# Mixture-of-experts stages on one core: weight rounding, `hidT` and row gathers in another order

## The reference, cut to what matters

```python
# top-1 of 4 groups, then top-2 of its 8 experts; pairs (token, expert)
# are sorted by expert into blocks of 128 rows, padded per expert
def run_block(args):
    xb, e = args                       # 128 rows x 1024
    hid = jax.nn.silu(xb @ w_gate[e]) * (xb @ w_up[e])     # 128 x 256
    return hid @ w_down[e]             # 128 x 1024
y = segment_sum(out[dest] * gate, token)   # added to the residual stream
```

## Time and profile before

| | us |
|---|---|
| median of three runs (3124.84 to 3132.12) | 3131.38 |
| the profiled execution | 3119.75 |
| its span in the profile | 3117.8 |
| expert stage of layer 0, about | 1188 to 1730 |
| expert stage of layer 1, about | 2588 to 3117 |

### The profile page before, as it was taken

The page is one execution under the profiler, slowest core; times in us unless marked ns, Lnnn a source line. Parts: engine busy times, 40 slices in busy tenths (PEclk is TensorE's granted clock), DMA queues, the critical chain, the costliest instruction groups (busy, mean ns, idle before and its releaser), DMA issues. The chain is left out here.

```text
span 3117.8 us, 48627 instructions
## 1 busy us (share of the span) xinstructions
PE 2673.4 (86%) x15109; PEld 2236.8 (72%) x15112; DVE 1747.1 (56%) x3154; ACT 1260.4 (40%) x2369; POOL 724.0 (23%) x923
## 2 busy tenths in 40 slices
PE   5999979997968947998898599799879947989997
PEld 4999958875847836777676488578658836767775
DVE  4222246665755665667765366588733354676664
ACT  3222132225841104556654222288611104675653
POOL 1000023321110002444343143211100002444433
PEclk9999989998988968999999799899979968999998
DMA  6111112215536516899997322222154415999995
GB/s 243 50 56 52 40 60 78 75 65 165 163 121 234 194 61 216 261 301 302 316 281 228 118 87 80 91 83 88 53 198 143 149 39 179 298 359 285 283 308 132
DMA packets 175389, 509.57 MB, mean 163 GB/s; under 512 B 53800, under 2 KB 81456, under 8 KB 150320
## 3 DMA queue, kind: packets, MB, share of 16 engines
q1 hardware_dynamic: 142480, 393.69, 34.7%
q0 software_dynamic: 32800, 114.51, 15.4%
HBM read 374.56 MB, written 133.56 MB: 163 GB/s over the span
## 5 line engine op out<-in xcount | busy, mean ns | idle before, releaser
L1700 DVE TENSOR_TENSOR moe_parts<-expert_w,moe_parts 128x1024 fp32r<-128x1024 f32 x384 | 452.3, 1221 | 238.4 <-ACT moe_parts L1649 234.9
L1582 PE MATMUL ps<-moe_parts,moe_xT 128*128 128x512 f32 x2232 | 551.6, 403 | 23.0 <-issue 16.0
L1582 PEld LDWEIGHTS ps<-moe_parts,moe_xT 128*128 128x128 f32 x2232 | 418.1, 191 | 125.3 <-issue 20.5
L1649 ACT ACTIVATE moe_parts<-expert_w 128x1024 fp32r<-128x1024 f32 x384 | 373.3, 1047 | 80.3 <-PEq L155 78.8
L1109 PE MATMUL ps<-out_w,out_catT 128*128 128x512 f32 x1344 | 322.4, 399 | 14.2 <-DVE out_w L1265 11.8
L560 PE MATMUL ps<-in_gate_w,in_gate_hnT 128*128 128x384 f32 (+1 forms) x1536 | 319.4, 367 | 7.4 <-DVE in_gate_w L679 7.4
L1582 PE MATMUL ps<-moe_parts,moe_hidT 128*128 128x512 f32 x1116 | 289.0, 408 | 26.9 <-DVE moe_hidT L1713 24.2
L560 PEld LDWEIGHTS ps<-in_gate_w,in_gate_hnT 128*128 128x128 f32 x1536 | 278.7, 190 | 37.4 <-issue 7.5
L1109 PEld LDWEIGHTS ps<-out_w,out_catT 128*128 128x128 f32 x1344 | 255.7, 192 | 69.4 <-DVE out_w L1265 12.6
L560 PE MATMUL ps<-in_qk_w,in_qk_hnT 128*128 128x512 f32 x1152 | 268.4, 394 | 9.2 <-DVE in_qk_w L679 9.2
L1582 PEld LDWEIGHTS ps<-moe_parts,moe_hidT 128*128 128x128 f32 x1116 | 205.7, 191 | 76.2 <-DVE moe_hidT L1713 32.8
(11 more groups left out here) (262 smaller groups left out, 4150.8 us busy)
## 6 DMA issues: line engine op xcount, KB each, us to landing
expert_w<-in_w_gate SPq DMA_DIRECT2D x64, 1024.0 KB
expert_w<-in_w_up SPq DMA_DIRECT2D x64, 1024.0 KB
expert_w<-in_w_down SPq DMA_DIRECT2D x64, 1024.0 KB
hn_d<-out_hn SPq DMA_DIRECT2D x32, 512.0 KB, 2.6
in_gate_xt<-in_x SPq DMA_DIRECT2D x16, 512.0 KB
in_qk_xt<-in_x SPq DMA_DIRECT2D x16, 512.0 KB
att_k<-k_d SPq DMA_DIRECT2D x64, 128.0 KB, 2.9
out_ht<-in_x SPq DMA_DIRECT2D x16, 512.0 KB, 4.6
```

Of the source, the lines that this page charges most:

```text
L1582: last = nc.tensor.matmul(out, left[:, a, k, :], right(b, k), start=(n == 0 and k == 0), stop=(n == 2 and k == K_ - 1))
L1649: nc.scalar.activation(parts[:, j, 0, at], K.expert_w[:, j, at], ACT.Copy).then_inc(w_high.sem, 1)
L1700: nc.vector.tensor_tensor(parts[:, j, 1, at], K.expert_w[:, j, at], parts[:, j, 0, at].bitcast(F32), ALU.subtract).then_inc(w_low.sem, 1)
```

## The change

- Weights: `load_expert` becomes `load_up` (gate and up) and `load_down`, each with its own semaphores. The down weights of an expert are split in that expert's own first block, no longer in the one before, and loaded accordingly.
- ScalarE's order in a block becomes `act(m-1)`, `x_out(m)`, `hid_out(m-1)`, `y_scaled(m-2)`, with the pieces of weights between them; the rounding of `hidT` is ScalarE's, the subtraction stays VectorE's.
- `raise_` and `lower` begin when the high part is there and wait for the low part before the last third of their matmuls.
- The gather takes its indices from `K.where` with a bounds check that drops rows past 2047; `K.who` is gone. `xg` is cleared once.
- `y_scaled` reads its gate straight from `K.gates`, which has a leading column of zeros; `set_gate` is gone. One extra `y_scaled(-1)` runs at the start and isn't scattered.

The core of the diff (the `who` and `gates` allocations, `load_up` and `load_down` themselves and unchanged lines are left out):

```diff
         def _(sp):
             def load(i, j):
 
-                load_expert(K, sp, layer, i * 2 + j, j, lambda n: alone(
-                    sp, w_low, i * (2 * PIECES) + ((j - 2) * PIECES + (n + 1) * PIECES // 3), K.tick_sp))
-            with sp.Fori(1, NE // 2) as i:
+                if not (isinstance(i, int) and i == 0 and j == 0):
+                    alone(sp, Count(d_low), (i * 2 + j) * D_PIECES, K.tick_sp)
+                    load_down(K, sp, layer, i * 2 + j + 1, 1 - j)
+                load_up(K, sp, layer, i * 2 + j + 2, j, lambda n: alone(
+                    sp, Count(gu_low), (i * 2 + j) * GU_PIECES + (n + 1) * GU_PIECES // 2, K.tick_sp))
+            for j in range(2):
+                load(0, j)
+            with sp.Fori(1, NE // 2 - 1) as i:
                 for j in range(2):
                     load(i, j)
+            alone(sp, Count(d_low), (NE - 2) * D_PIECES, K.tick_sp)
+            load_down(K, sp, layer, NE - 1, 1)
             if layer == 0:
 
-                sp.wait_ge(w_low.sem, NE * PIECES)
+                sp.wait_ge(gu_low, NE * GU_PIECES)
+                sp.wait_ge(d_low, NE * D_PIECES)
                 sp.dma_start(K.w_in_odd, K.x["w_in_odd"].rearrange("a (p k) n -> p (a k) n", k=DK)).then_inc(K.weights_in[5], 16)
...
             def gather(m):
-                nc.gpsimd.tensor_copy(who[:, :], K.who[:, m:m + 1] if isinstance(m, int) else K.who[:, bass.ds(m, 1)]).then_inc(who_set.sem, 1)
+                nc.gpsimd.tensor_copy(who[:, :], K.where[:, m:m + 1] if isinstance(m, int) else K.where[:, bass.ds(m, 1)]).then_inc(who_set.sem, 1)
                 alone(g, who_set, m + 1, K.tick)
                 nc.gpsimd.indirect_dma_start(xg[:, :], None, K.hn_d[layer],
-                                             bass.IndirectOffsetOnAxis(ap=who[:, :], axis=0)).then_inc(gathered_s, 16)
-
-            def set_gate(m):
-                nc.gpsimd.tensor_copy(gate[:, :], K.gates[:, bass.ds(m, 1)]).then_inc(gated.sem, 1)
+                                             bass.IndirectOffsetOnAxis(ap=who[:, :], axis=0),
+                                             bounds_check=T - 1, oob_is_err=False).then_inc(gathered_s, 16)
...
+            g.memset(xg[:, :], 0.0).then_inc(cleared, 1)
+            g.wait_ge(cleared, 1)
             gather(0)
 
-            g.dma_start(where[:, :], K.where[:, 0:1]).then_inc(scattered_s, 16)
+            for n in range(2):
+                g.dma_start(where[:, :], K.where[:, 0:1]).then_inc(scattered_s, 16)
+                g.wait_ge(scattered_s, 16 * (n + 1))
...
             with g.Fori(1, total) as m:
-                set_gate(m - 1)
-
                 alone(g, x_turned, m + 2, K.tick)
                 gather(m + 2)
                 scatter(m - 1)
-            set_gate(total - 1)
...
-            def product(out, left, right, K_):
-
-                for n, (a, b) in enumerate(((0, 0), (0, 1), (1, 0))):
+            def product(out, left, right, K_, terms):
+
+                for a, b in terms:
                     for k in range(K_):
-                        last = nc.tensor.matmul(out, left[:, a, k, :], right(b, k), start=(n == 0 and k == 0),
-                                                stop=(n == 2 and k == K_ - 1))
+                        last = nc.tensor.matmul(out, left[:, a, k, :], right(b, k), start=(a + b + k == 0),
+                                                stop=(a == 1 and k == K_ - 1))
                 return last
...
             def raise_(m, j):
 
                 wgu = parts[:, j, :, 0:GU].rearrange("p h (s k f) -> p h k s f", s=2, k=DK)
+                until(pe, x_high, m + 1)
+
+                until(pe, hid_done, m)
+                product(gup, xT, lambda h, k: wgu[:, h, k, :, :], DK, ((0, 0), (0, 1)))
                 until(pe, x_low, m + 1)
...
             def lower(m, j):
 
                 wd = parts[:, j, :, GU:EW].rearrange("p h (k n) -> p h k n", k=2)
-                until(pe, h_low, m + 1)
-                until(pe, y_out, m)
-                for half in range(2):
-                    last = product(yp[:, 512 * half:512 * (half + 1)], hidT,
-                                   lambda h, k: wd[:, h, k, 512 * half:512 * (half + 1)], 2)
+                until(pe, h_high, m + 1)
+                until(pe, y_out, m + 1)
+                for terms in (((0, 0), (0, 1)), ((1, 0),)):
+                    if terms[0][0] == 1:
+                        until(pe, h_low, m + 1)
+                    for half in range(2):
+                        last = product(yp[:, 512 * half:512 * (half + 1)], hidT,
+                                       lambda h, k: wd[:, h, k, 512 * half:512 * (half + 1)], 2, terms)
                 last.then_inc(down.sem, 1)
...
-                pe.wait_ge(w_low.sem, i * (2 * PIECES) + j * PIECES + GU_PIECES)
+                pe.wait_ge(gu_low, i * (2 * GU_PIECES) + (j + 1) * GU_PIECES)
                 raise_(m, j)
                 turn_x(m + 1)
                 if behind:
+                    pe.wait_ge(d_low, i * (2 * D_PIECES) + j * D_PIECES)
                     lower(m - 1, 1 - j)
-                pe.wait_ge(w_low.sem, i * (2 * PIECES) + (j + 1) * PIECES)
...
+            def block_(i, j, m):
                 turn_hid(m - 1)
                 raise_(m, j)
                 turn_x(m + 1)
+                pe.wait_ge(d_low, i * (2 * D_PIECES) + (j + 1) * D_PIECES)
                 lower(m - 1, j)
+            pe.sem_inc(down.sem, down.credit)
             turn_x(0)
             in_turn(pe, first_block, block_)
             total = end_of(pe, NE)
             turn_hid(total - 1)
+            pe.wait_ge(d_low, NE * D_PIECES)
             lower(total - 1, 1)
...
+            def split_up(j, pieces):
                 for n in pieces:
                     at = slice(n * PIECE, (n + 1) * PIECE)
-                    nc.scalar.activation(parts[:, j, 0, at], K.expert_w[:, j, at], ACT.Copy).then_inc(w_high.sem, 1)
+                    nc.scalar.activation(parts[:, j, 0, at], K.expert_w[:, j, at], ACT.Copy).then_inc(gu_high, 1)
+
+            def split_down(i, j):
+                a.wait_ge(K.down_in[layer][j], i * 16 + 16)
+                for n in range(GU_PIECES, GU_PIECES + D_PIECES):
+                    at = slice(n * PIECE, (n + 1) * PIECE)
+                    nc.scalar.activation(parts[:, j, 0, at], K.expert_w[:, j, at], ACT.Copy).then_inc(d_high, 1)
...
+            def hid_out(m):
+                until(a, h_turned, m + 1)
+                nc.scalar.activation(hidT[:, 0, :, :], hp.rearrange("p (k c) -> p k c", k=2), ACT.Copy).then_inc(h_high.sem, 1)
+
             def y_scaled(m):
                 until(a, down, m + 1)
-                until(a, gated, m + 1)
-
-                a.wait_ge(scattered_s, m * 16 + 16)
-                nc.scalar.activation(y[:, :], yp, ACT.Copy, scale=gate[:, 0:1]).then_inc(y_out.sem, 1)
+
+                a.wait_ge(scattered_s, m * 16 + 32)
+                column = K.gates[:, m + 1:m + 2] if isinstance(m, int) else K.gates[:, bass.ds(m + 1, 1)]
+                nc.scalar.activation(y[:, :], yp, ACT.Copy, scale=column).then_inc(y_out.sem, 1)
 
             def first_block(i, j, m, behind, ahead):
                 ni, nj = i + j, 1 - j
+                if behind:
+                    act(m - 1)
                 if ahead:
-
-                    a.wait_ge(K.expert_in[layer][nj], ni * 48 + 48)
-                    if behind:
-                        until(a, up, m)
-                    split(ni, nj, range(GU_PIECES))
-                act(m)
-                x_out(m + 1)
+                    a.wait_ge(K.up_in[layer][nj], ni * 32 + 32)
+                    split_up(nj, (0,))
+                x_out(m)
                 if behind:
-                    y_scaled(m - 1)
+                    hid_out(m - 1)
                 if ahead:
-                    split(ni, nj, range(GU_PIECES, PIECES))
-
-            def block_(m, j):
-                act(m)
-                x_out(m + 1)
-                y_scaled(m - 1)
-            a.wait_ge(K.expert_in[layer][0], 48)
-            split(0, 0, range(PIECES))
-            x_out(0)
+                    split_up(nj, (1,))
+                if behind:
+                    y_scaled(m - 2)
+                split_down(i, j)
+                if ahead:
+                    split_up(nj, range(2, GU_PIECES))
+
+            def block_(i, j, m):
+                act(m - 1)
+                x_out(m)
+                hid_out(m - 1)
+                y_scaled(m - 2)
+            a.wait_ge(K.up_in[layer][0], 32)
+            split_up(0, range(GU_PIECES))
             in_turn(a, first_block, block_)
-            y_scaled(end_of(a, NE) - 1)
+            total = end_of(a, NE)
+            act(total - 1)
+            hid_out(total - 1)
+            y_scaled(total - 2)
+            y_scaled(total - 1)
 
         @block.vector
         def _(v):
             v.sem_inc(hid_done.sem, hid_done.credit)
 
-            def split(i, j, pieces):
-
+            def rest(j, n, done):
```

(46 more changed lines are left out.)

50 lines of the change are left out of this document (20 added, 30 removed).

## The result

The kernel after takes 3156.44 us in the median (3147.94 to 3157.27) beside 3128.11 for the kernel before measured next to it, a ratio of 1.0096 with the 95% interval [1.0078, 1.0114]. I had forecast 3109 us, with a range that ended at 3144. The profiled execution has a span of 3145.8 us beside 3117.8: 28 us more.

The account below looks back on a forecast made before the run. TensorE and the DMA engines were each taken to bound some blocks, DMA in runs of one-block experts. Terms -14 - 2 + 0 - 3 + 3 - 2.4 - 5 + 1 = -22.4 us from 3131.4 gave 3109 us, range 3065 to 3144.

Parts of the forecast that it names:

- the part on the weights: Expert weight loads: three go out within about 2.5 us, runs stay above about 11.5 us a block; cost against today nothing.
- The term for two-block experts: Blocks of the 29 two-block experts, from ScalarE's and VectorE's work: 0 us, bounds -6 to +15.
- The order of work: Expert stages: `hidT` and issue waits of 35.4 us lose their cause; credited -14 us for 14 one-block experts, -2 for others.
- rival 1: Expert stages: DMA engines already the limit, `hidT` waits return as waits for weights or rows; some -6 us, 3125; chance 0.20.
- `hidden` in two-block experts: VectorE's `hidden(m)` ends at +12.6, `turn_hid(m)` wants it at 13.0: 0.4 us of room.
- The gather: Gather of rows: dropped padding rows gain 3 us (bounds 0 to 20), the bounds check costs 0.05 us each, 3 us.
- Start: Start of both layers: the second `raise_` no longer needs the 1.2 us subtraction of x; -2.4 us in all.
- Tail: Layer 0's 8.91 us gather wait goes, but `w_in_odd` slows scatters: -5 us (0 to -8.9); `hid_out` before y, both tails: +1.
- The copies of the indices: GpSimd's index copies beside VectorE subtractions stay long: nothing gained, up to about 0.5 us lost for each.
- My one slower case: Checked gather issues 0.6 us slower on 60 blocks, +36 us, total 3142; decides from about 0.37 us; chance 0.14.
- Rival 3: Expert stages: loops open fully, DMA time found in two-block experts; about -60 us, 3071; chance 0.15.
- what I had named as signs: Profile after: `hidT` and x waits gone, lone one-block experts from 12 to 10 or 11 us, runs near 12, no 9 us tail wait.

Follow-up runs that it names:

- e6: The kernel after without the weight loads inside the stage, experts using the first two experts' weights: 3029.13 us, with three blocks more than the kernel before.
- e1: The kernel after with the gather of before: indices from `K.who`, no bounds check, padding fetched again: 3161.87 us, 1.0126 of before.
- e4: The kernel before with the changed gather alone: indices from `K.where`, bounds check, padding dropped, `xg` cleared once: 3129.89 us, 1.0023 of before.

## Why the prediction was wrong, point by point

**The failed step** is in the part on the weights: "The three loads now go out within about 2.5 us, at +9.9 to +12.2" was read rightly from the code (2.2 us in the trace), and then "It costs nothing against today". I asked only when the weights would be there for ScalarE, and never who else was on the DMA engines at +9.9 to +12.2. The next gather of a full block is issued at just that time. The material was there: the share of 0.87 in the two-block stretch is a mean over unequal parts (by the periods of before in layer 0, 0.95 in second blocks and 0.73 in the first blocks behind them), and in the part on the gather I wrote that 36.7 us of waits say that the loop has no room. A price of 0 for putting 1 MB more beside it doesn't agree with that. It measured +69 us over the 25 second blocks. The term for two-block experts, 0 with bounds of -6 to +15, was bounded by VectorE's and ScalarE's work alone, and its upper end was too low by the same omission; so was the whole range.

**The order of work** was right in mechanism, sized too low and put in the wrong place: -16 us against -32 over all first blocks. I credited 14 us to one-block experts that stand alone or begin a run. They had no `hidT` wait to lose and stayed at 9.8 us. The gain came in the first blocks of two-block experts that follow a one-block expert, which I had not credited. What I said of runs held: inside them 11.84 us, not below 11.5, at a DMA share of 1.02. There rival 1 describes what happened. e6 shows 3.0 us for each block behind a one-block expert where no load stands in the way.

**`hidden` in two-block experts**, the layout with 0.4 us of room, held: 1.1 us of waits in the middle of layer 0, the longest 0.6.

**The gather** (-3 and +3): by e1 and after, check and dropped rows together gain 0.3% with intervals that overlap; by e4 and before they lose 0.2%. Small, as forecast, and of no settled sign.

**Start** (-2.4): the two starts are 5 us shorter. **Tail** (-5 + 1): from layer 0's last `raise_` to its last scatter it takes 27.4 us where it took 30.2. No transpose waits for 9 us:

```profile
1716.27 1.04 PE L1596 MATMUL ps<-ident,moe_xg 128*128 128x128 f32 x8
...
1736.21 0.19 POOL L1553 COPY moe_where<-where 128x1 int32 x1 [12.02 <-DMA h_d<-moe_y,moe_where]
1738.05 1.58 POOL L1556 DMA_INDIRECT h_d<-moe_y,moe_where  x1 [1.65 <-ACT moe_y L1685]
```

but GpSimd waits 12.02 us in its place for the last scatter but one, with `w_in_odd` beside it, as the text said it might. **The copies of the indices** take 180/186/1036 ns where they took 181/314/1161: the long ones are rarer, so the loss that the rule of the Trainium skill (GPSIMD Engine Reference, Key points) allowed for didn't come. That dropping **`set_gate`** gained nothing is not shown by a run of its own.

**The rivals.** My one slower case was the check's instruction, with a price and a point from which it decides, and its price was ten times too high (0.6 and 0.06 us). (Rival 3's terms add up to about -63 us, not -60; nothing hangs on it.) The right one, that loads moved together delay the transfer which TensorE waits for, was a sentence away. Of what I had named as signs, most came true (the waits for `hidT` and x gone but for one of 0.6 us, runs near 12 us at a share near 1, no tail wait), and the time went the other way. They were signs for the step I had costed, and said nothing of the one that I hadn't. One sign was misread from the start: lone one-block experts took 9.8 us before and after, not 12 and 10 or 11.

What stays open: what decides whether a wait also costs clock, and what holds a gather's rows back for its first 4.7 us beside loads. One-block experts inside a run of layer 0 take 11.8 us with 3 MB, 10.4 with 2, 10.3 with 1 and 9.9 without loads; with 3 MB the DMA engines are full (1.02), but with 1 MB they aren't (0.72), and there TensorE waits for `hidden` instead (10.0 us in ten waits from 1206 to 1620).

## What to carry to other kernels

When a change moves a load, write down which other transfer is in flight at its new time and how much slack that one has, not only whether the moved load is in time for its own user. A load that was spread over the block and becomes a burst uses no more bandwidth, and yet delays whatever is queued on another queue: here the third megabyte cost 2.6 us a second block, and moving it behind the gather turned +0.96% into -0.4%. The cost starts where the slack ends: compare when the transfer lands with when it is wanted. And where an engine's wait is removed, measure the floor of both orders without the traffic: it tells what the order is worth (47 us in a layer) and what the traffic hides or takes back.

## What the hardware showed that I had not expected

- A gather of up to 128 rows of 4 KB lands in 4.4 us in the median without loads. Beside loads its queue moves hardly anything in the first 4.7 us (0.06 and 0.14 MB, with scatters in it) and then shares the engines with the weight queue by packets: 36.4% to 64.8% where 3 MB were queued, 91.7% to 12.1% where that queue had nearly run dry.
- Behind a wait of 2.8 us TensorE ran at a granted clock of 0.61 and 0.74 for 5 us, which cost 1.8 us more; behind one of 3.1 us in the same layer it cost 0.3.
- The bounds check adds 0.06 us to the gather's instruction (median 1067 ns for 1005) and really drops the rows: 17.3 MB less on the queue.
